# Latent attention with the plain and the rotated parts of queries and keys in tiles of their own

## The chip, the cores and the metric

The kernel runs on one core of one Trainium2 chip. The metric is the time on the device in microseconds (us), the median of several runs. All data are float32.

## What is computed

The reference is a model of three blocks over 512 tokens of width 1024; only the mixer of the last block matters here. It projects the normalised tokens to a compressed query `cq` (384), a compressed key and value `ckv` (256), a rotated key `kr` (32, shared by all heads), the queries, keys and values of a dilated attention, and two gates. Latent attention over 8 heads, and the merge behind it, cut from the reference:

```
q = (rms_norm(cq, q_norm_g) @ w_uq).reshape(B, S, 8, 64 + 32)
q = concatenate([q[..., :64], rope(q[..., 64:])])
k_rope = rope(kr)                                    # one for all heads
k_nope = (c_kv @ w_uk).reshape(B, S, 8, 64)
v_a    = (c_kv @ w_uv).reshape(B, S, 8, 64)
k_a = concatenate([k_nope, broadcast(k_rope)])
o_a = dense_attention(q, k_a, v_a)                   # softmax(q k / sqrt(96)) v, no mask
merged = gates[0] * (o_a @ w_branch_a) + gates[1] * (o_b @ w_branch_b)
return merged @ w_out
```

## The kernel before

One program with an instruction stream written out by hand for each engine; the engines meet by counting semaphores (`wait_ge`, `then_inc`). Activations lie transposed, 128 channels by 512 tokens a tile. Weights come through a ring of six units of 1 MB, loaded by SyncE in a fixed order (`mixer_units` for the mixer). `lin_open` takes the two PSUM banks 0 and 1 in turn, and waits until VectorE has emptied the tile before last (`lin_free`). Every logical float32 product is issued as two matmul instructions.

The order around the change: the input projections of the mixer (lines 1147 to 1177), dilated attention (1179 to 1188), the projections of latent attention (1191 to 1216), its attention loop (1219 to 1230), the product with the second branch's weights (`branch`, 1232), and the output projection.

Projections of latent attention: `head_query` (1191) makes one head's 96 query rows with three logical products; VectorE copies them to `HT[0:96, h]` (line 1379) and, two heads behind, rotates them with `rope` (1396 to 1405, a shuffle and three tensor operations over all 96 rows, with an angle of zero in the plain rows). Four key tiles (1212), two heads each, are copied in two halves to `KT` (2223, 2225). GpSimd copies the rotated key under each of the eight heads' plain keys (2882). The values are four token tiles of two logical products each (524), copied by 1392.

The attention loop (`attention`, 738) has 32 jobs: for each pair of heads, four blocks of 128 queries, and the two heads in turn. A job is: scores (one logical product over 96 rows, line 1222, into bank 4 + job mod 4); their maximum on VectorE (1561, 1571); exponentials on ScalarE (2458), which free the bank; a reciprocal and a scaling on VectorE (1581, 1584); four transposes on TensorE (760, `turn`); and their copy by ScalarE (2471). Two jobs' scores are issued ahead, in front of the transposes of the even job. VectorE takes the maximum of job u+1, then scales job u, then takes what a fill or a pair of heads left (`take_done`, 1599). Behind every eight jobs, a pair of heads is multiplied with its values (810, two column groups side by side), one job into the next eight; ScalarE's copy of the first transposes of the next heads waits for it. `fill` puts a tile of the product with the first branch's weights (539, eight instructions) in front of the transposes of jobs 3, 7, ..., 31; VectorE multiplies it with its gate (1461).

In the dilated attention the loop is the same, with scores of 64 rows, even heads in partitions 0 to 63 and odd ones in 64 to 127 (1181), and with half a gate tile (554, eight instructions) in front of every job's transposes.

```
                        if u % 2 == 0 and u + 2 < len(jobs):
                            scores(u + 2)
                            scores(u + 3)
                        if u or not lead:
                            fill(u)
                        if u % (2 * TT) == 1 and u > 2 * TT:
                            head_pair_values(u // (2 * TT) - 1)
                        turn(u)
```

Of the kernel before, what the change touches and what calls it, by code (L numbers as in the profile page):

```python
# [20 lines left out]
P = 128  # L21
# [24 lines left out]
DA_BRANCH = (12, 13, 14, 14, 15)  # L46
FF = 2816
# [118 lines left out]
def shape_constants():  # L166
# [21 lines left out]
    freq[64:80, 2] = -inv3  # L188
    freq[80:96, 2] = inv3
# [18 lines left out]
def build_program(nc, A, out):  # L208
    with ExitStack() as ctx:
# [30 lines left out]
        CQ, CKV, KR, ROPEM = BIG[:, 0:3, :], BIG[:, 3:5, :], BIG[0:DQK, 5, :], BIG[:, 6:8, :]  # L240
        KT, VA, MB = BIG[:, 16:24, :], BIG[:, 8:12, :], BIG[:, 0:8, :]
# [180 lines left out]
        def _(pe):  # L422
# [83 lines left out]
            def project(w, nk, width, rhs, ring_name, m=P, h_wait=False):  # L506
# [231 lines left out]
            def attention(heads, score, nkeys, ahead, maps, values, taken, fill, lead=None):  # L738
# [5 lines left out]
                def scores(u):  # L744
# [7 lines left out]
                    mm.then_inc(Q["sc_ready"], now.inc("sc_ready"))  # L752

# [23 lines left out]
                for u in range(ahead):  # L777
                    scores(u)
                for u in range(len(jobs)):
# [7 lines left out]
                    else:  # L787
                        if u % 2 == 0 and u + 2 < len(jobs):
                            scores(u + 2)
                            scores(u + 3)  # L790
                        if u or not lead:
                            fill(u)
                        if u % (2 * TT) == 1 and u > 2 * TT:
                            head_pair_values(u // (2 * TT) - 1)
                        turn(u)
                if maps == 2:
                    head_values(heads - 1)
                else:
                    head_pair_values(heads // 2 - 1)
# [360 lines left out]
            project(unit(), KD, 96, HT, "lin_ready", m=96)  # L1160
# [30 lines left out]
            def head_query(w, h):  # L1191
                wv = w[:, 0:3 * 384].rearrange("p (k c) -> p k c", k=3)
                ps = lin_open()
                for k in range(3):
                    mm = pe.matmul(ps[0:DQK, :], wv[:, k, h % 4 * DQK:(h % 4 + 1) * DQK], CQ[:, k, :],
                                   start=k == 0, stop=k == 2)
                mm.then_inc(Q["lin_ready"], now.inc("lin_ready"))

            w = unit()
            for h in range(4):  # L1200
                head_query(w, h)
            unit_used("lin_ready")
            w = unit()
            for h in range(4, 8):
                head_query(w, h)
                if h == 7:
                    unit_used("lin_ready")
            w = unit()[:, 0:2 * 512].rearrange("p (k c) -> p k c", k=2)
            for t in range(4):
                ps = lin_open()  # L1210
                for k in range(2):
                    mm = pe.matmul(ps, w[:, k, t * P:(t + 1) * P], CKV[:, k, :], start=k == 0, stop=k == 1)
                mm.then_inc(Q["lin_ready"], now.inc("lin_ready"))
                if t == 3:
                    unit_used("lin_ready")
            project_tokens(unit(), 2, 512, CKV)
            pe.wait_ge(Q["kr_copied"], now.next("kr_copied", MLA_H))

            def mla_score(o, h, m, qb):
                if qb == 0:  # L1220
                    pe.wait_ge(Q["roped"], KR_ROPES + h + 1)
                return pe.matmul(o, HT[0:DQK, h, qb * P:(qb + 1) * P], KT[0:DQK, h, :], start=True, stop=True)
# [6 lines left out]
            at["mla"] = now.count("lin_ready")  # L1229
# [10 lines left out]
        def _(v):  # L1240
# [306 lines left out]
            def attention(heads, nkeys, maps, scale, mask, L, head_done, take_fill, between=lambda u: None, sooner=()):  # L1547
# [50 lines left out]
                maxima(0)  # L1598
                def take_done(u):
# [569 lines left out]
            store_scaled(BIG[:, 5:6, :], 1, rows=DQK)  # L2169
# [30 lines left out]
            for s in range(2):  # L2200
                quarter_sums(g + 4 + s, quarters=token_quarters(DV, s))
                scale_tokens(DV, s)
                if s == 0:
                    rope(KR, SWAP_16, ROPEM[0:DQK, 0, :], ROPEM[0:DQK, 1, :], TURN[0:DQK, 0:S])
# [8 lines left out]
            def rope_head(h):  # L2213
                rope(HT[0:DQK, h, :], SWAP_16, ROPEM[0:DQK, 0, :], ROPEM[0:DQK, 1, :], TMP[0:DQK, 0, :])
# [5 lines left out]
            for t in range(MLA_H // 2):  # L2220
                ps = lin_take()
                v.wait_ge(*now.prev())
                v.tensor_copy(KT[0:HD, 2 * t, :], ps[0:HD, :]).then_inc(Q["dve_step"], now.inc("dve_step"))
                v.wait_ge(*now.prev())
                v.tensor_copy(KT[0:HD, 2 * t + 1, :], ps[HD:P, :]).then_inc(Q["lin_free"], now.inc("lin_free"))
                if t % 2:
                    rope_head(6 + t // 2)
            store_tokens(VA, 1, 512)
            v.wait_ge(Q["g_exp"], now.next("g_exp", 2 * KD))

            def take_branch_fill(u):
                if u % 4 == 3:
                    first_branch(MB, u // 4, KD + u // 4)
            attention(MLA_H, lambda qb: S, 1, float(DQK) ** -0.5, None, 0, pair_done(HT), take_branch_fill)
# [36 lines left out]
        def _(act):  # L2271
# [418 lines left out]
            mla = fill_order(MLA_H, 1, lambda u: u % 4 == 3)  # L2690
# [28 lines left out]
        def _(pool):  # L2719
# [158 lines left out]
            pool.wait_ge(Q["pos2_landed"], 32)  # L2878
# [157 lines left out]
```

## Time and profile before

| | us |
|---|---|
| median of three runs | 3076.05 |
| lowest and highest of them | 3075.49, 3081.58 |
| the profiled execution | 3078.61 |
| its span in the trace | 3076.9 |
| TensorE busy | 2957.9 (96%) |
| VectorE busy | 1326.0 (43%) |
| ScalarE busy | 652.8 (21%) |
| GpSimd busy | 844.5 (27%) |

The span is that of the instructions; the execution's own time is 1.7 us longer. In the page and its views PE is TensorE and PEld its weight loads, which run beside its matmuls; DVE is VectorE, ACT ScalarE, POOL GpSimd. L1222 is line 1222 of the kernel. Matmuls are pipelined: one of 512 columns lasts 0.59 us in the records, but the next starts 0.43 us after it. A number in brackets at the end of a row is the time for which the engine sat idle before it, and what released it. PEclk is the clock granted to TensorE, as a share of full speed.

### The profile page before, as it was taken

What the parts mean: (1) busy time and instruction counts of PE and PEld (TensorE: products, weight loads), DVE (VectorE), ACT (ScalarE), POOL (GpSimd) and SP (SyncE); (2) the same over time, 40 slices, a digit from 0 to 9 for tenths busy, and PEclk for the clock granted to TensorE, in tenths of its full rate; (3) what the DMA queues carried; (4) which work ended last, traced back from release to release, by engine and by line L of the source; (5) the groups of instructions that cost most, each with busy time, mean ns of one, the idle gap of its engine ahead of it and who ended that gap; (6) DMA issues with size and microseconds to landing.
All of it is one profiled execution on the core that took longest, in us unless ns stands there. A gap on an engine that the chain in (4) does not pass through costs nothing.

```text
span 3076.9 us, 31525 instructions
## 1 busy us (share of the span) xinstructions
PE 2957.9 (96%) x12406; PEld 1865.7 (61%) x12406; DVE 1326.0 (43%) x2202; ACT 652.8 (21%) x1055; POOL 844.5 (27%) x641
## 2 busy tenths in 40 slices
PE   9999998999999999989998999999999999999998
PEld 7865464333468654633333688887664345688887
DVE  6733543111546335431224644443563564544442
ACT  2035313111210253231112300002112341300011
POOL 5400021322134000222222154443400002345442
PEclk9999999999999999999999999999999999999999
DMA  4211124999522101249996122222221111122220
GB/s 185 83 69 42 42 88 181 389 384 386 217 82 83 69 28 55 74 148 384 379 379 276 69 93 85 82 96 82 91 77 45 68 42 55 69 83 96 82 96 28
DMA packets 81380, 412.65 MB, mean 134 GB/s; under 512 B 25872, under 2 KB 26256, under 8 KB 34768
## 3 DMA queue, kind: packets, MB, share of 16 engines
q1 hardware_dynamic: 56608, 387.54, 33.2%
q0 software_dynamic: 24624, 23.08, 2.3%
q8 instruction: 99, 1.62, 0.2%
q14 instruction: 49, 0.40, 0.0%
HBM read 513.28 MB, written 31.46 MB: 177 GB/s over the span
## 4 chain that ended last, share of the span: by engine, by line
PE 86%; DVE 8%; ACT 4%; issue 1%; DMA 1%; POOL 0%; SPq 0%; DVEq 0%; ACTq 0%; POOLq 0%
PE PS L998 37%; PE PS L937 11%; PE PS L554 6%; PE PS L539 5%; PE PS L959 5%; PE PS L628 4%; PE PS L514 3%; PE PS L1138 3%; PE PS L911 1%; PE PS L760 1%; PE PS L810 1%; PE PS L477 1%; PE PS L819 1%; PE PS L703 1%; DVE ATT L1511 1%
## 5 line engine op out<-in xcount | busy, mean ns | idle before, releaser
L2814 POOL TENSOR_TENSOR ATT<-ring 128x512 f32<-128x512 f32 (+1 forms) x98 | 129.4, 1320 | 1138.5 <-PE PS L998 710.7
L998 PE MATMUL PS<-G,ring 128*128 128x256 f32 x1360 | 321.6, 379 | 0.0
L998 PE MATMUL PS<-G,ATT 128*128 128x256 f32 x1232 | 291.4, 379 | 0.0
L998 PE MATMUL PS<-HT,ring 128*128 128x256 f32 x1264 | 287.6, 379 | 3.4 <-ACT HT L2367 1.8
L998 PEld LDWEIGHTS PS<-G,ring 128*128 128x128 f32 x1360 | 258.4, 190 | 35.1
L998 PEld LDWEIGHTS PS<-HT,ring 128*128 128x128 f32 x1264 | 239.7, 190 | 40.3 <-issue 4.0
L2538 ACT ACTIVATE TMP<-PS 128x256 f32<-128x256 f32 x92 | 35.3, 384 | 1053.5 <-PE PS L998 936.2
L998 PEld LDWEIGHTS PS<-G,ATT 128*128 128x128 f32 x1232 | 234.1, 190 | 32.7 <-issue 0.7
L937 PE MATMUL PS<-ring,G 128*64 128x512 f32 x1024 | 226.8, 595 | 2.5 <-ACT G L2507 2.5
L554 PE MATMUL PS<-HT,ring 128*128 128x512 f32 x448 | 205.4, 601 | 0.0
L2822 POOL TENSOR_TENSOR ATT<-ring 128x512 f32<-128x512 f32 (+1 forms) x98 | 173.4, 1769 | 7.7
L1839 DVE TENSOR_TENSOR G<-PS,G 128x256 f32<-128x256 f32 x48 | 20.4, 424 | 343.5 <-ACT G L2513 343.3
L998 PE MATMUL PS<-HT,ATT 128*128 128x256 f32 x696 | 164.6, 379 | 0.0
L1910 DVE TENSOR_TENSOR BIG<-PS,TMP 128x256 f32<-128x256 f32 x100 | 42.4, 424 | 260.5 <-ACT TMP L2538 257.6
L937 PEld LDWEIGHTS PS<-ring,G 128*64 128x64 f32 x1024 | 70.7, 137 | 135.9 <-issue 132.9
L998 PEld LDWEIGHTS PS<-HT,ATT 128*128 128x128 f32 x696 | 132.1, 190 | 18.3 <-issue 0.5
L554 PEld LDWEIGHTS PS<-HT,ring 128*128 128x128 f32 x448 | 80.7, 190 | 101.6 <-issue 96.2
L1910 DVE TENSOR_TENSOR G<-PS,TMP 128x256 f32<-128x256 f32 x42 | 17.8, 424 | 270.1 <-ACT TMP L2538 265.1
L2816 POOL TENSOR_TENSOR ATT<-ring 128x512 f32<-128x512 f32 (+1 forms) x98 | 133.5, 1363 | 0.0
L2756 POOL DMA_INDIRECT expert_rows<-G,ATT x46 | 46.6, 1013 | 311.0 <-DVE G L1850 310.6
L2819 POOL TENSOR_TENSOR ring<-ATT,ring 128x512 f32<-128x512 f32 (+1 forms) x98 | 128.8, 1314 | 7.7
L959 PE MATMUL PS<-ring,G 128*64 128x512 f32 x512 | 116.0, 594 | 10.2 <-DVE G L1832 5.9
(363 smaller groups left out, 4483.9 us busy)
## 6 DMA issues: line engine op xcount, KB each, us to landing
ring<-in_stream SPq DMA_DIRECT2D x163, 1024.0 KB, 4.8
ring<-in_experts_gu SPq DMA_DIRECT2D x128, 1024.0 KB, 8.8
ring<-in_experts_down SPq DMA_DIRECT2D x64, 1024.0 KB, 8.7
G<-expert_rows SPq DMA_DIRECT2D x8, 1024.0 KB, 7.6
h_tokens<-G POOLq DMA_DIRECT2D x2, 2048.0 KB, 7.6
XT<-in_xT SPq DMA_DIRECT2D x1, 1024.0 KB, 8.7
G<-in_pT POOLq DMA_DIRECT2D x2, 512.0 KB, 6.3
out_T<-XT SPq DMA_DIRECT2D x2, 512.0 KB, 3.7
```

The source lines that it names most:

```text
L514: mm = pe.matmul(ps[0:m, :], wv[:, k, c:c + m], rhs[:, k, :], start=k == 0, stop=k == nk - 1)
L539: mm = pe.matmul(ps, w[:, k, c:c + P], rhs[:, k, :], start=k == 0, stop=k == nk - 1)
L554: mm = pe.matmul(units["ps"], w[:, k, c:c + P], rhs[:, k, :], start=k == 0, stop=k == KD - 1)
L628: mm = pe.matmul(product(g, name), y[:, k, s * P:(s + 1) * P], x[:, k * 256:(k + 1) * 256], start=k == 0 and name in ("P1", "P2", "P3", "P ...
L937: mm = pe.matmul(PS[r, 4 + q % 2, :], XGT[:, q % 2, k * P + CAP * side:k * P + CAP * (side + 1)], ws[side][:, kk * 512:(kk + 1) * 512], st ...
L959: mm = pe.matmul(PS[r, n, :], HIDT[:, q % 2, j * P + CAP * side:j * P + CAP * (side + 1)], ws[side][:, j * D + n * 512:j * D + (n + 1) * 512],
L998: mm = pe.matmul(product(g, name), x[:, k * P:(k + 1) * P], y[:, k, :], start=first and k == 0 and name in ("P1", "P2", "P3", "P5"), stop= ...
L1138: mm = pe.matmul(ps, w[:, k, m % 2 * P:(m % 2 + 1) * P], HP[:, k, :], start=k == 0, stop=k == KD - 1)
L2814: pool.tensor_tensor(a["S1"], a["A21"], a["A22"], ALU.add)\
L2816: pool.tensor_tensor(a["S3"], a["A11"], a["A21"], ALU.subtract)\
L2819: pool.tensor_tensor(a["S2"], a["S1"], a["A11"], ALU.subtract)\
L2822: pool.tensor_tensor(a["S4"], a["A12"], a["S2"], ALU.subtract)\
```

## The change

The weights of the queries are reordered on the host into a unit of rotated columns (8 heads by 32) and a unit of plain columns (8 heads by 64). The queries become two tiles of rotated rows (`QT`, four heads each) and four of plain rows (`QN`, two heads each); keys become four plain tiles (`KN`) and one tile `KEY` that holds the rotated key four times over, once in each 32 rows (the key's columns are repeated in its weights). The scores of a job are two products that add up in PSUM: 64 plain rows and 32 rotated rows, and `two_scores` issues the plain products of two jobs, then the rotated ones. The values are projected behind the first two jobs' scores (`early`). The fills go in front of the transposes of the jobs in `MLA_BRANCH`, the last behind the transposes of job 31. The first tile of the second branch waits for the last heads only in front of its last product.

```diff
+MLA_BRANCH = (4, 9, 13, 17, 21, 25, 29, 31)
...
 def mixer_units(w_in, w_uq, w_uk, w_uv, w_a, w_b, w_o):
+    key = np.tile(w_in[:, QR + KVR:QR + KVR + ROPE_M], (1, P // ROPE_M))
+    heads = w_uq.reshape(QR, MLA_H, DQK)
+    turned = heads[:, :, NOPE:].reshape(QR, MLA_H * ROPE_M)
+    plain = heads[:, :, :NOPE].reshape(QR, MLA_H * NOPE)
...
-         unit_of(w_in, 0, D, 576, 672)]
+         unit_of(key, 0, D, 0, P)]
...
-    return (u + cut(w_uq, 384) + cut(w_uk, 512) + cut(w_uv, 512)
+    return (u + cut(turned, MLA_H * ROPE_M) + cut(plain, MLA_H * NOPE) + cut(w_uk, 512) + cut(w_uv, 512)
...
-        CQ, CKV, KR, ROPEM = BIG[:, 0:3, :], BIG[:, 3:5, :], BIG[0:DQK, 5, :], BIG[:, 6:8, :]
-        KT, VA, MB = BIG[:, 16:24, :], BIG[:, 8:12, :], BIG[:, 0:8, :]
+        CQ, CKV, KR, ROPEM = BIG[:, 0:3, :], BIG[:, 3:5, :], BIG[:, 5, :], BIG[:, 6:8, :]
+        KN, VA, MB = BIG[:, 16:20, :], BIG[:, 8:12, :], BIG[:, 0:8, :]
+        QN, QT, KEY = HT[:, 0:4, :], HT[:, 4:6, :], HT[:, 6, :]
...
+                        if late and c == 0 and k == nk - 1:
+                            pe.wait_ge(*late)
...
+                def two_scores(u):
+                    for part in score:
+                        for n in (u, u + 1):
+                            if part is score[0] and n >= 4:
+                                pe.wait_ge(Q[taken], base[taken] + n - 3)
+                            h, qb = jobs[n]
+                            mm = part(PS[:, 4 + n % 4, 0:nkeys(qb)], h, 0, qb)
+                            if part is score[-1]:
+                                mm.then_inc(Q["sc_ready"], now.inc("sc_ready"))
...
-                for u in range(ahead):
-                    scores(u)
+                if early:
+                    two_scores(0)
+                    early()
+                else:
+                    for u in range(ahead):
+                        scores(u)
...
-                            scores(u + 2)
-                            scores(u + 3)
-                        if u or not lead:
+                            if early:
+                                two_scores(u + 2)
+                            else:
+                                scores(u + 2)
+                                scores(u + 3)
+                        last = early and u == len(jobs) - 1
+                        if (u or not lead) and not last:
                             fill(u)
                         if u % (2 * TT) == 1 and u > 2 * TT:
                             head_pair_values(u // (2 * TT) - 1)
                         turn(u)
+                        if last:
+                            fill(u)
...
-            project(unit(), KD, 96, HT, "lin_ready", m=96)
+            project(unit(), KD, P, HT, "lin_ready")
...
-            w = unit()
-            for h in range(4):
-                head_query(w, h)
...
-            project_tokens(unit(), 2, 512, CKV)
-            pe.wait_ge(Q["kr_copied"], now.next("kr_copied", MLA_H))
...
+            project(unit(), 3, MLA_H * ROPE_M, CQ, "lin_ready")
+            project(unit(), 3, MLA_H * NOPE, CQ, "lin_ready")
+            project(unit(), 2, MLA_H * NOPE, CKV, "lin_ready")
+
+            def plain_score(o, h, m, qb):
+                r = slice(NOPE * (h % 2), NOPE * (h % 2 + 1))
+                return pe.matmul(o, QN[r, h // 2, qb * P:(qb + 1) * P], KN[r, h // 2, :], start=True, stop=False)
+
+            def turned_score(o, h, m, qb):
+                if qb == 0 and h == 0:
+                    pe.wait_ge(Q["kr_copied"], now.next("kr_copied"))
+                if qb == 0 and h % 4 == 0:
+                    pe.wait_ge(Q["roped"], KR_ROPES + h // 4 + 1)
+                r = slice(ROPE_M * (h % 4), ROPE_M * (h % 4 + 1))
+                return pe.matmul(o, QT[r, h // 4, qb * P:(qb + 1) * P], KEY[r, :], start=False, stop=True)
...
-                if u % 4 == 3:
-                    project_tile(b, 4, 512, DQ, u // 4)
+                if u in MLA_BRANCH:
+                    project_tile(b, 4, 512, DQ, MLA_BRANCH.index(u))
...
-            attention(MLA_H, mla_score, lambda qb: S, 2, 1, pair_values(VA), "e_ready", branch_fill)
-            drained("lin_ready")
-            branch(HT[:, 0:4, :])
+            attention(MLA_H, (plain_score, turned_score), lambda qb: S, 2, 1, pair_values(VA), "e_ready", branch_fill,
+                      early=lambda: project_tokens(unit(), 2, 512, CKV))
+            paired = now.count("lin_ready")
+            project(unit(), 4, 512, HT[:, 0:4, :], "lin_ready", late=(Q["lin_free"], paired))
+            project(unit(), 4, 512, HT[:, 0:4, :], "lin_ready")
...
                 maxima(0)
+                if early:
+                    early()
...
-            for h in range(MLA_H):
-                store(HT[:, h:h + 1, :], 1, rows=DQK)
-                if h >= 2:
-                    rope_head(h - 2)
...
+            store(QT, 2)
+            for i in range(2):
+                rope(QT[:, i, :], SWAP_16, ROPEM[:, 0, :], ROPEM[:, 1, :], TMP[:, 0, :])
+                store(QN[:, 2 * i:2 * i + 2, :], 2)
+            store(KN, MLA_H // 2)
...
-            for h in range(MLA_H):
-                pool.tensor_copy(KT[NOPE:DQK, h, :], KR[NOPE:DQK, :]).then_inc(Q["kr_copied"], now.inc("kr_copied"))
+            pool.tensor_copy(KEY, KR).then_inc(Q["kr_copied"], now.inc("kr_copied"))
```

The angles of the rotation are laid out for all four groups of 32 rows, and VectorE takes the fills, and the values' four tiles (behind the maximum of job 0), in the order of TensorE.

## Rows read from the trace of the kernel before

**Rows 1.** Page, part 1: busy time and share of the span of each engine.
```profile
PE 2957.9 (96%) x12406; PEld 1865.7 (61%) x12406; DVE 1326.0 (43%) x2202; ACT 652.8 (21%) x1055; POOL 844.5 (27%) x641
```
**Rows 2.** Window view: length, busy us of PE, PEld, DVE, ACT, POOL; clock, DMA share.
```profile
2426.70:2474.30 47.60, 38.03 (x82) 13.84 (x81) 36.67 (x61) 10.66 (x14) 4.49 (x8) 0.96 0.19 66
2474.30:2568.70 94.40, 87.75 (x320) 41.57 (x320) 56.14 (x140) 44.03 (x96) 0.00 (x0) 0.98 0.10 34
```
**Rows 3.** Timeline of VectorE, a query head: start, us, engine, line, operation.
```profile
2438.42 0.69 DVE L1379 COPY HT<-PS 96x512 f32<-96x512 f32 x1
...
2439.15 0.72 DVE L1399 STREAM_SHUFFLE TMP<-HT 96x512 f32<-96x512 f32 x1
...
2442.14 0.69 DVE L1379 COPY HT<-PS 96x512 f32<-96x512 f32 x1
```
**Rows 4.** Timeline of TensorE: a query head that waited, and the first transposes.
```profile
2442.88 2.81 PE L1195 MATMUL PS<-BIG,ring 128*96 128x512 f32 x6 [0.49 <-DVE HT L1379]
...
2478.22 0.66 PE L760 MATMUL PS<-MATS,ATT 128*128 128x128 f32 x4 [0.23 <-DVE ATT L1584]
```
**Rows 5.** Timeline of TensorE, dilated attention: transposes, scores, gate tile, transposes.
```profile
2294.89 0.60 PE L760 MATMUL PS<-MATS,ATT 128*128 128x128 f32 x4
2295.42 1.13 PE L1181 MATMUL PS<-BIG 64*128 64x512 f32 x4
2296.48 3.70 PE L554 MATMUL PS<-HT,ring 128*128 128x512 f32 x8
2300.02 0.60 PE L760 MATMUL PS<-MATS,ATT 128*128 128x128 f32 x4
```
**Rows 6.** Timeline of TensorE, latent attention, jobs 8 to 13.
```profile
2497.60 0.60 PE L760 MATMUL PS<-MATS,ATT 128*128 128x128 f32 x4
2498.13 3.65 PE L810 MATMUL PS<-ATT,BIG 128*64 128x512 f32 x16
2501.72 0.66 PE L760 MATMUL PS<-MATS,ATT 128*128 128x128 f32 x4
2502.21 1.88 PE L1222 MATMUL PS<-BIG,HT 96*128 96x512 f32 x4
2504.23 0.63 PE L760 MATMUL PS<-MATS,ATT 128*128 128x128 f32 x4
2504.70 3.60 PE L539 MATMUL PS<-BIG,ring 128*128 128x512 f32 x8
2508.13 0.60 PE L760 MATMUL PS<-MATS,ATT 128*128 128x128 f32 x4
2508.57 1.88 PE L1222 MATMUL PS<-BIG,HT 96*128 96x512 f32 x4
2510.29 0.60 PE L760 MATMUL PS<-MATS,ATT 128*128 128x128 f32 x4
2511.44 0.63 PE L760 MATMUL PS<-MATS,ATT 128*128 128x128 f32 x4 [0.55 <-DVE ATT L1584]
```
**Rows 7.** Timeline of ScalarE and VectorE: a copy behind the values product, a maximum.
```profile
2501.88 0.60 ACT L2471 ACTIVATE ATT<-PS 128x512 f32<-128x512 f32 x1 [4.31 <-PE PS L810]
...
2509.63 0.69 DVE L1561 TENSOR_REDUCE SM<-PS 128x1 f32<-128x512 f32 x1 [0.41 <-PE PS L1222]
```
**Rows 8.** Window view, columns as in group 2: jobs 29 and 30, and behind them.
```profile
2554.80:2558.20 3.40, 1.64 (x11) 1.11 (x10) 2.13 (x7) 2.75 (x6) 0.00 (x0) 1.00 0.00 0
2558.30:2561.70 3.40, 3.40 (x5) 1.35 (x4) 0.51 (x2) 0.51 (x1) 0.00 (x0) 0.50 0.00 0
```
**Rows 9.** Timeline of TensorE, the end of latent attention and the second branch.
```profile
2557.87 5.29 PE L539 MATMUL PS<-BIG,ring 128*128 128x512 f32 x8
2563.00 0.60 PE L760 MATMUL PS<-MATS,ATT 128*128 128x128 f32 x4
2564.29 3.65 PE L810 MATMUL PS<-ATT,BIG 128*64 128x512 f32 x16 [0.69 <-ACT ATT L2471]
2568.74 0.70 PE L514 MATMUL PS<-HT,ring 128*128 128x512 f32 x1 [0.79 <-DVE HT L1626]
```

More of the change, by code:

```diff
@@ L187, in shape_constants @@
             freq[b + h:b + h + 8, 1] = sign * inv2
-    freq[64:80, 2] = -inv3
-    freq[80:96, 2] = inv3
+    for b in range(0, P, ROPE_M):
+        freq[b:b + 16, 2] = -inv3
+        freq[b + 16:b + 32, 2] = inv3
     rev = np.zeros((P, NG + NE), np.float32)
@@ L504, in late_sum, with project @@
                     .then_inc(Q["late_sum"], now.inc("late_sum"))
-            def project(w, nk, width, rhs, ring_name, m=P, h_wait=False):
+            def project(w, nk, width, rhs, ring_name, m=P, h_wait=False, late=None):
                 wv = w[:, 0:nk * width].rearrange("p (k c) -> p k c", k=nk)
@@ L736, in stick_breaking, with attention @@
                 now.skip("w_ready", SB_H)
-            def attention(heads, score, nkeys, ahead, maps, values, taken, fill, lead=None):
+            def attention(heads, score, nkeys, ahead, maps, values, taken, fill, lead=None, early=None):
                 jobs = attention_jobs(heads, maps)
@@ L1189, in _ @@
             pe.wait_ge(Q["h_ready"], now.next("h_ready", (QR + KVR) // P))
[L1191 to L1197, printed above, removed]
-            w = unit()
@@ L1200, in _ @@
-            for h in range(4):
-                head_query(w, h)
[L1202 to L1215, printed above, removed]
@@ L1216, in _ @@
-            project_tokens(unit(), 2, 512, CKV)
-            pe.wait_ge(Q["kr_copied"], now.next("kr_copied", MLA_H))
[L1219 to L1222, printed above, removed]
+            project(unit(), 3, MLA_H * ROPE_M, CQ, "lin_ready")
+            project(unit(), 3, MLA_H * NOPE, CQ, "lin_ready")
+            project(unit(), 2, MLA_H * NOPE, CKV, "lin_ready")
@@ L1224, in _ @@
             b = {}
             def branch_fill(u):
-                if u % 4 == 3:
-                    project_tile(b, 4, 512, DQ, u // 4)
-            at["mla"] = now.count("lin_ready")
-            attention(MLA_H, mla_score, lambda qb: S, 2, 1, pair_values(VA), "e_ready", branch_fill)
-            drained("lin_ready")
-            branch(HT[:, 0:4, :])
+                if u in MLA_BRANCH:
+                    project_tile(b, 4, 512, DQ, MLA_BRANCH.index(u))
+            at["mla"] = now.count("lin_ready") + TT
@@ L1545, in stick_breaking, with attention @@
                 now.skip("lw_ready", SB_H)
-            def attention(heads, nkeys, maps, scale, mask, L, head_done, take_fill, between=lambda u: None, sooner=()):
+            def attention(heads, nkeys, maps, scale, mask, L, head_done, take_fill, between=lambda u: None, sooner=(), early=None):
                 jobs = attention_jobs(heads, maps)
@@ L2168, in _ @@
             store_scaled(CKV, 2)
-            store_scaled(BIG[:, 5:6, :], 1, rows=DQK)
+            store_scaled(BIG[:, 5:6, :], 1)
             begin_sum("lin_free", QR // P + KVR // P + 1)
@@ L2203, in _ @@
                 if s == 0:
-                    rope(KR, SWAP_16, ROPEM[0:DQK, 0, :], ROPEM[0:DQK, 1, :], TURN[0:DQK, 0:S])
+                    rope(KR, SWAP_16, ROPEM[:, 0, :], ROPEM[:, 1, :], TURN[:, 0:S])
             def take_gate_fill(u):
@@ L2212, in _ @@
             at["dil_done"] = now.count("lin_free")
-            def rope_head(h):
-                rope(HT[0:DQK, h, :], SWAP_16, ROPEM[0:DQK, 0, :], ROPEM[0:DQK, 1, :], TMP[0:DQK, 0, :])
-            for h in range(MLA_H):
-                store(HT[:, h:h + 1, :], 1, rows=DQK)
-                if h >= 2:
-                    rope_head(h - 2)
[L2220 to L2229, printed above, removed]
-            def take_branch_fill(u):
-                if u % 4 == 3:
-                    first_branch(MB, u // 4, KD + u // 4)
-            attention(MLA_H, lambda qb: S, 1, float(DQK) ** -0.5, None, 0, pair_done(HT), take_branch_fill)
+            store(QT, 2)
[3 more added lines that the diff above has]
+            store(KN, MLA_H // 2)
+            def take_branch_fill(u):
+                if u in MLA_BRANCH:
+                    m = MLA_BRANCH.index(u)
+                    if m == 0:
+                        v.wait_ge(Q["g_exp"], now.next("g_exp", 2 * KD))
+                    first_branch(MB, m, KD + m)
+            attention(MLA_H, lambda qb: S, 1, float(DQK) ** -0.5, None, 0, pair_done(HT), take_branch_fill,
+                      early=lambda: store_tokens(VA, 1, 512))
             at["mla_done"] = now.count("lin_free")
@@ L2689, in _ @@
             dil = fill_order(MLA_H, 1, lambda u: u % 2)
-            mla = fill_order(MLA_H, 1, lambda u: u % 4 == 3)
+            mla = fill_order(MLA_H, 1, lambda u: u in MLA_BRANCH)
             attention(MLA_H, lambda qb: S, 1, 1.0, True,
```

1 line of the change is left out of this document (removed).

## The prediction

> **What bounds the kernel now.** I read the page first: TensorE is busy 2957.9 us, 96% of the span [rows 1], so an edit counts only where it shortens or lengthens what TensorE issues, or where it starts or ends a wait of TensorE. Then the window view of the two stages that the diff touches. In the projections of latent attention, 2426.7 to 2474.3, TensorE is busy 38 of 47.6 us; in the attention loop, up to the second branch, 87.8 of 94.4 us [rows 2]. The first stage has slack that isn't TensorE's. The VectorE timeline says why: one head of the queries costs it a copy and a four-step rotation, 3.72 us from copy to copy (2438.42 to 2442.14) [rows 3], while TensorE needs six instructions of 0.43 us, 2.6 us; it starts the next head when VectorE has freed a bank: the product at 2442.88 waited for the copy that began at 2442.14 [rows 3, 4]. So VectorE sets the pace there. In the loop TensorE mostly sets it, with waits for the softmax of the next job where nothing stands in front of its transposes: 2510.29 to 2511.44 where 0.44 would do [rows 6].
>
> **The projections.** Removed: eight heads of six instructions, replaced by two rotated and four plain tiles of six each; the four key tiles (four instructions each) stay; the values' 16 instructions go behind the first scores. That leaves 52 instructions by 0.43, 22.4 us. VectorE has 10 copies by 0.73 (the step from copy to shuffle [rows 3]) and two rotations by 3.0 (3.72 less the copy), 13.3 us: it no longer sets the pace, and each rotation stands where two banks cover it. The wait for the last copy stays, about 1 us (0.79 is idle and some 0.2 is uncovered behind the last heads' copy [rows 9]). The first scores then start at 2426.7 + 22.4 + 1.0 = 2450.1, where now they start at 2474.3.
> GpSimd copies the rotated key once instead of eight times, and starts when the dilated heads are copied, 20 us before the first scores need it. The key unit has 128 columns instead of 96: still 16 instructions, and copies of 96 rows take 0.69 us [rows 3], as those of 128 do. Units of weights and DMAs stay equal in number. All this at nothing.
>
> **The opening of the loop.** Scores of jobs 0 and 1, 2.1 us; the values, 16 by 0.43, 6.9; then jobs 2 and 3 beside VectorE's last value copy, the maximum of job 1 and the scaling of job 0: 0.2 + 0.73 + 1.0 + 0.8 = 2.7 us. The first transpose comes at 2450.1 + 2.1 + 6.9 + 2.7 = 2461.8, where now it comes at 2478.2 [rows 4]: **16.4 us earlier**.
>
> **The scores.** Now a pair of jobs is four instructions, 1.72 us (2508.57 to 2510.29) [rows 6]. After, it is a pair of 64-row products and a pair of 32-row products. The 64-row form is in the trace: the dilated branch's scores take two row groups side by side, four instructions in 1.06 us, and with them transposes to transposes take 5.13 us (2294.89 to 2300.02) [rows 5], against 0.44 + 3.43 = 3.87 without [rows 6]. So the pair costs 1.26: two steps of 0.43, and 0.40 for two changes of tile height, 0.20 each. If the 32-row pair runs side by side too, a pair of jobs costs 0.86 + 0.86 + 3 x 0.20 = 2.32 us, 0.60 more than now. Nothing in the trace goes from 64 rows straight to 32: between nothing and 0.30, I take the 0.20 of the other two changes. Both ends stay in the range: 16 pairs, 3.2 us less or 1.6 more.
> The Trainium skill (TensorEngine Tiling (Array Packing), Key Properties) says that a change of tiling mode, not of the tile alone, drains TensorE; this case's trace agrees for 128 to 64 and back, 0.20 us each, and by the rule the third change costs the same; without it the forecast would be 3 us lower.
> Fourteen pairs lie behind the first transpose: 14 x 0.60 = **8.4 us more**.
>
> **The waits in the loop.** Of jobs u and u+1 (u even), the transposes of u+1 need VectorE to have taken the maximum of job u+2 first, since that stands ahead in its queue. From that maximum to the transposes it is 1.81 us (2509.63 to 2511.44) [rows 6, 7]. Now the score of u+2 is ready 0.86 us before its partner's, and the wait is 0.71. After, both of a pair end together, so the maximum starts some 0.1 us behind the start of job u's transposes: u+1 starts 1.9 us after u, a wait of 1.45. And there are more such places. A weight product stands in front of jobs 3, 7, 11, ... now, and a values product in front of 9, 17, 25; what is bare is 5, 13, 21. The new list puts the products in front of 9, 13, 17, ..., in three cases right beside the values product; bare are 3, 7, 15, 23 and 11, 19, 27. At the last three VectorE also has two copies to do (branch tile and heads, 0.73 each) ahead of the maximum, behind a scaling that itself waited for ScalarE, which waits out the values product (4.31 us [rows 7]): about 2.4 us each. After: 4 x 1.45 + 3 x 2.4 = 13.0. Before: 3 x 0.71, and three times 0.30 behind the values product (2502.21 to 2504.23 less 1.72) [rows 6], 3.0, the latter now covered by longer scores. Jobs 30 and 31 wait about 2 us either way. Difference **10.0 us more**.
>
> **The end.** The last weight product moves behind the last transposes, where the values now wait 1.29 - 0.53 = 0.8 us, and three quarters of the first branch tile run before the last heads are copied, where 4.45 - 3.59 = 0.9 us is idle [rows 6, 9]. **1.7 us less.** VectorE and GpSimd start their next work with the same copy, so later stages only shift.
>
> **The clock.** The last weight product took 5.13 us (2557.87 to 2563.00) [rows 9] instead of 3.43: for 3.4 us the granted clock was 0.50, right behind a stretch in which TensorE was busy 1.64 of 3.40 us [rows 8]. That 1.7 us goes, as the jobs shift; but the new bare places (three of 2.4 us, the end, the opening) are as thin. Between none and five dips; I take two, at 1.7 each, since a dip needs the thin part to fall right: net **1.7 us more**.
>
> **Sum.** -16.4 + 8.4 + 10.0 - 1.7 + 1.7 = +2.0 us. The profiled execution took 3078.6 us, so 3080.6 for it; the median of the runs shown is 3076.05, 2.6 lower, and there I forecast 3078.1. A measurement of this kernel can tell about 0.2%, 6.2 us, from no change: this is no change, the gain of the projections given back in the loop. The case's own range: no third change of height and no dip, 3076.05 + 2.0 - 3.2 - 3.4 = 3071.5; the dear change and five dips, 3076.05 + 2.0 + 1.6 + 5.1 = 3084.7.
>
> **Rivals.** Faster: the loop hides what it gains in work. If successive products of different height follow without a change, and the copies of VectorE fall before the three long waits (each then 1.45), the sum is -16.4 + 7.1 - 1.7 - 1.7 = -12.7, 3063 us. For it: the pace of now has slack on VectorE (56 of 94 us busy [rows 2]). Against: the 0.20 is plain in the trace, and the order of VectorE's queue is fixed.
> Slower, first: the change doesn't do what it says, and the 32-row pair does not run side by side. Then each pair costs 0.86 more, 16 x 0.86 = 13.8, which no wait absorbs, as VectorE's wait counts from their end: 3092 us. It decides once over half of the pairs run in turn (7 us). For it: no 32-row product is in the trace. Against: the 64-row ones pair perfectly.
> Slower, second: the thin places make the clock fall each time: five dips instead of two, and with a dear third change 3084. The trace has it once in a like place.
>
> **How the numbers follow.** Forecast 0.50, faster rival 0.25, 32 rows in turn 0.12, clock 0.13. Faster by over 0.2% (below 3069.9): the rival and 0.02 of the forecast's low end, 0.27. Slower (above 3082.2): the other two and a little, 0.26. The likeliest case alone is 3071.5 to 3084.7; the range goes from 3061, under the faster rival, to 3087, and leaves out the row groups in turn and little else.
>
> **What would show it.** Right: the projections end near 2449 with TensorE without a gap; a score pair of eight instructions takes 2.3 us; job 11's transposes wait 2.4 us behind VectorE's copies; the second branch starts at about its old time, near 2567. Wrong: score pairs near 1.8 or 3.2 us, or transposes of jobs 3, 7, 11 that do not wait.

## The result, and the profile after

The changed kernel took 3088.64 us (median of seven runs, 3082.44 to 3090.14), beside 3076.17 us for the kernel before in the same runs. The ratio is 1.0032, with a 95% interval of 1.0022 to 1.0042: **slower by about 10 us** (the two medians alone lie 12.5 us apart). On the median of 3076.05 shown ahead of the prediction the ratio gives 3085.9 us (3082.8 to 3089.0); the forecast was 3078.1 us in a range of 3061 to 3087. That is inside the range, 1.1 us below its upper end, with an interval that reaches past it, and outside the likeliest case of 3071.5 to 3084.7. No change was forecast and a small loss came; the rival of the falling clock is what happened, at a higher price than I gave it.

The page of the changed kernel, its span, part 1 and the clock of part 2, answers to [rows 1]:

```profile
span 3086.1 us, 31578 instructions
PE 2966.5 (96%) x12458; PEld 1865.9 (60%) x12458; DVE 1307.0 (42%) x2166; ACT 652.4 (21%) x1055; POOL 840.8 (27%) x634
PEclk9999999999999999999999999999999989999999
```

VectorE has 19 us less to do, as intended, and TensorE is 9 us longer busy with 52 more instructions of 12,458. The windows of the projections up to the first scores, and of the loop from the first transposes to the second branch, answer to [rows 2]. The columns are length, busy us of PE, PEld, DVE, ACT and POOL, mean clock, and DMA:

```profile
2423.40:2446.80 23.40, 22.55 (x54) 9.76 (x53) 13.21 (x21) 10.63 (x14) 0.61 (x1) 1.00 0.26 90
2458.60:2577.00 118.40, 102.71 (x369) 42.53 (x369) 53.12 (x133) 42.44 (x92) 0.00 (x0) 0.88 0.06 22
```

Of the kernel before, the projections are the 47.6 us of [rows 2], which hold the values' 16 instructions as well, and the loop alone is this window:

```profile
2478.20:2568.70 90.50, 84.08 (x312) 40.14 (x312) 53.79 (x134) 42.48 (x92) 0.00 (x0) 0.98 0.07 24
```

The projections are pure TensorE now (22.55 of 23.40 us busy). The loop grew from 90.5 to 118.4 us, and its mean clock fell from 0.98 to 0.88. The granted clock was at half for 27.3 us of it, in four falls of 3.4 to 10.2 us, where before there was one of 3.4 [rows 8]. The first four windows here lie within these falls, which began in or just behind the waits of jobs 11, 15, 19 and 23 (columns as above):

```profile
2493.20:2500.00 6.80, 6.80 (x15) 2.47 (x14) 3.40 (x11) 2.60 (x6) 0.00 (x0) 0.50 0.00 0
2507.00:2510.20 3.20, 3.20 (x10) 1.37 (x11) 1.29 (x4) 1.48 (x5) 0.00 (x0) 0.50 0.00 0
2524.20:2534.20 10.00, 9.61 (x21) 4.24 (x22) 4.72 (x13) 3.01 (x8) 0.00 (x0) 0.50 0.00 0
2541.20:2547.80 6.60, 6.60 (x15) 2.56 (x14) 2.99 (x8) 1.19 (x3) 0.00 (x0) 0.50 0.02 4
2559.80:2566.40 6.60, 6.60 (x24) 2.96 (x25) 4.43 (x12) 2.75 (x6) 0.00 (x0) 1.00 0.00 0
```

The last line is the stretch behind job 27, which waits 2.52 us like jobs 11 and 19: the clock stays full there, as it does behind jobs 1, 3, 7 and 31.

What it looks like from job 8 to job 13, in the timeline of TensorE, beside [rows 6] (L1226 plain products, L1234 rotated ones, L779 transposes, L548 branch tile, L839 values):

```profile
2478.90 0.66 PE L779 MATMUL PS<-MATS,ATT 128*128 128x128 f32 x4
2479.40 3.60 PE L548 MATMUL PS<-BIG,ring 128*128 128x512 f32 x8
2482.93 3.65 PE L839 MATMUL PS<-ATT,BIG 128*64 128x512 f32 x16
2486.51 0.66 PE L779 MATMUL PS<-MATS,ATT 128*128 128x128 f32 x4
2487.10 1.13 PE L1226 MATMUL PS<-BIG,HT 64*128 64x512 f32 x4
2488.16 1.13 PE L1234 MATMUL PS<-HT 32*128 32x512 f32 x4
2489.22 0.66 PE L779 MATMUL PS<-MATS,ATT 128*128 128x128 f32 x4
2492.39 0.63 PE L779 MATMUL PS<-MATS,ATT 128*128 128x128 f32 x4 [2.52 <-DVE ATT L1598]
2492.95 1.84 PE L1226 MATMUL PS<-BIG,HT 64*128 64x512 f32 x4
2494.72 2.08 PE L1234 MATMUL PS<-HT 32*128 32x512 f32 x4
2496.73 1.11 PE L779 MATMUL PS<-MATS,ATT 128*128 128x128 f32 x4
2497.63 4.81 PE L548 MATMUL PS<-BIG,ring 128*128 128x512 f32 x8
2502.28 0.60 PE L779 MATMUL PS<-MATS,ATT 128*128 128x128 f32 x4
```

Job 11's transposes (2492.39) wait 2.52 us for VectorE; behind that wait the same score pair that took 2.12 us (2487.10 to 2489.22) takes 3.78 (2492.95 to 2496.73), and the branch tile 4.65 instead of 3.43. The timeline of VectorE shows what stands ahead of the maximum of job 12 (2490.57), behind a scaling (2488.39) that was late itself:

```profile
2488.20 0.16 DVE L1595 RECIPROCAL SM<-SM 128x1 f32<-128x1 f32 x1 [6.55 <-ACT ATT L2466]
2488.39 0.49 DVE L1598 TENSOR_SCALAR ATT<-ATT,SM 128x512 f32<-128x512 f32 x1
2488.99 0.69 DVE L1475 TENSOR_TENSOR BIG<-PS,G 128x512 f32<-128x512 f32 x1
2489.78 0.69 DVE L1643 COPY HT<-PS 128x512 f32<-128x512 f32 x1
2490.57 0.69 DVE L1575 TENSOR_REDUCE SM<-PS 128x1 f32<-128x512 f32 x1
```

### The profile page after: what moved, and what is told of

It is laid out like the page before. It is cut to its first block, busy times and chain, and to the rows that moved or that the text cites. A ratio compares the mean times of both kernels' runs of the same rounds, so it can differ in the third digit from the quotient of the medians.

```text
span 3086.1 us, 31578 instructions
## 1 busy us (share of the span) xinstructions
PE 2966.5 (96%) x12458; PEld 1865.9 (60%) x12458; DVE 1307.0 (42%) x2166; ACT 652.4 (21%) x1055; POOL 840.8 (27%) x634
## 4 chain that ended last, share of the span: by engine, by line
PE 87%; DVE 7%; ACT 4%; issue 1%; DMA 1%; POOL 0%; SPq 0%; DVEq 0%; ACTq 0%; POOLq 0%
PE PS L1027 37%; PE PS L966 11%; PE PS L563 6%; PE PS L548 6%; PE PS L988 5%; PE PS L523 4%; PE PS L637 4%; PE PS L1167 3%; PE PS L940 1%; PE PS L779 1%; PE PS L839 1%; PE PS L484 1%; PE PS L848 1%; PE PS L712 1%; DVE ATT L1525 1%
```

## The experiments

Two theories stood after the result. A: the new list of fills leaves TensorE bare in front of too many odd jobs; the waits cost time themselves, and the thin stretches bring the clock down. B: it is the new score products, of 64 and 32 rows, that bring the clock down, whatever stands around them.

A table first. The loop is from the first transposes (job 0) to the first instruction of the second branch; "waits" is TensorE's time behind VectorE's scaling, with the wait of job 0, from the view of waits; "half" is the time in the loop at half clock, added up from windows of 0.5 us; the clock is the mean of the loop. These columns are of one profile each. The ratio is to the kernel before, in the same runs. Below, differences are between medians; from the changed kernel they come out 2 to 4 us smaller by the ratios (experiment 2: 9 instead of 12.7), since its ratio of 1.0032 is smaller than that of the two medians, 1.0041.

| kernel | median us | ratio (95% interval) | loop us | waits us | half us | clock |
|---|---|---|---|---|---|---|
| before | 3076.2 | | 90.5 | 4.8 | 3.4 | 0.98 |
| changed | 3088.6 | 1.0032 (1.0022 to 1.0042) | 118.4 | 16.1 | 27.3 | 0.88 |
| 1 old list | 3074.7 | 0.9994 (0.9985 to 1.0003) | 102.1 | 8.4 | 10.2 | 0.95 |
| 2 bare places filled | 3076.0 | 1.0003 (0.9994 to 1.0012) | 105.2 | 0.7 | | 1.00 |
| 3 before, new list | 3088.3 | 1.0041 (1.0028 to 1.0055) | 100.9 | 12.8 | 6.8 | 0.97 |
| 4 unpaired scores | 3140.6 (one run) | | 164.0 | 2.3 | 92.2 | 0.72 |
| 5 halves | 3061.9 | 0.9953 (0.9939 to 0.9966) | 91.4 | 2.6 | | 1.00 |
| 6 halves, copies moved | 3060.4 | 0.9948 (0.9935 to 0.9962) | 89.2 | 1.3 | | 1.00 |
| 7 before, halves | 3073.5 | 0.9991 (0.9982 to 1.0000) | 86.0 | 1.7 | | 1.00 |
| 8 copies moved alone | 3078.9 | 1.0007 (0.9997 to 1.0016) | 106.5 | 12.3 | 10.2 | 0.95 |
| 9 halves, values first | 3061.8 | 0.9953 (0.9937 to 0.9970) | 91.4 | 2.8 | | 1.00 |
| 10 filled, 32 rows | 3086.5 | 1.0033 (1.0020 to 1.0045) | 117.0 | 0.4 | 20.5 | 0.91 |

**1. The old list of fills on the changed kernel.**

```diff
-MLA_BRANCH = (4, 9, 13, 17, 21, 25, 29, 31)
+MLA_BRANCH = (3, 7, 11, 15, 19, 23, 27, 31)
```

> The changed kernel with the fills back in front of jobs 3, 7, 11, ..., 27 (the last stays behind job 31's transposes). Theory A (the list leaves TensorE bare in front of too many odd jobs, and the bare places lower the clock): the waits before jobs 3, 7, 11, 15, 19, 23, 27 go, those before 5, 13, 21, 29 come: some 7 us less waiting, and with thin places of 1.3 us only, most of the 27 us at half clock go, worth up to 13 us. 3065 to 3071 us, faster than before. Theory B (the score products of 64 and 32 rows, whatever stands around them, bring the clock down): only the 7 us of waits go and the half clock stays: 3079 to 3082 us.

It fell between the two theories: 3074.66 us, 14 less than the changed kernel, but no faster than before. The waits halved (7.7 us less), and the clock rose from 0.88 to 0.95, 17 us less at half clock. Two falls remain, behind job 13 and behind jobs 29 to 31; behind job 13 one bare job with a wait of 1.26 us was enough:

```profile
2497.03 0.65 PE L779 MATMUL PS<-MATS,ATT 128*128 128x128 f32 x4
2498.95 0.63 PE L779 MATMUL PS<-MATS,ATT 128*128 128x128 f32 x4 [1.26 <-DVE ATT L1598]
2499.51 2.08 PE L1226 MATMUL PS<-BIG,HT 64*128 64x512 f32 x4
2501.51 2.08 PE L1234 MATMUL PS<-HT 32*128 32x512 f32 x4
```

So the list is the larger part of the loss, and a wait as short as this can be followed by a fall. It need not be: jobs 5 and 21 wait 1.26 us in the same profile, and the clock stays full behind them.

**2. The bare places filled with idle products.** The results are overwritten by the transposes that follow, so the output stays.

```diff
+BARE = {1: (512,), 3: (512, 256), 7: (512, 256), 15: (512, 256), 23: (512, 256),
+        11: (512,) * 3, 19: (512,) * 3, 27: (512,) * 3, 31: (512, 512)}
...
+                    if early:
+                        for width in BARE.get(u, ()):
+                            pe.matmul(PS[:, 2 + u % 2, 0:width], IDENT, KN[:, 0, 0:width], start=True, stop=True)
                     pe.wait_ge(Q["p_ready"], now.next("p_ready"))
```

> The changed kernel with idle products (identity by a key tile, result overwritten by the transposes) in front of the transposes of the bare jobs, sized to the waits seen in the trace: 1 to 3 logical products of 0.86 us. Nothing else moves and no wait on VectorE gets shorter. Theory A: TensorE has no thin place left, the clock stays at full, and the time falls by what the half clock cost beside nothing else, 10 to 13 us, to 3075 to 3079 us. Theory B: the score products are as they were, so the clock still falls: 3086 to 3092 us. If I mis-sized the fillers, at most 2 us more.

3075.95 us, 12.7 less. Hardly anything but the clock's fall was made shorter: a filled job starts at most 0.1 us sooner than a bare one, some 0.5 us over the loop. The window of the loop:

```profile
2457.60:2562.80 105.20, 104.69 (x408) 44.45 (x408) 53.13 (x133) 42.44 (x92) 0.00 (x0) 1.00 0.07 25
```

The clock is full throughout, with the same score products. The half clock thus cost 118.4 - 105.2 = 13.2 us of the loop, near half of its 27.3 us. Theory A holds, and B in its strict form (whatever stands around them) falls.

**3. The new list on the kernel before.**

```diff
-                if u % 4 == 3:
-                    project_tile(b, 4, 512, DQ, u // 4)
+                if u in MLA_BRANCH:
+                    project_tile(b, 4, 512, DQ, MLA_BRANCH.index(u))
```

(and the same for VectorE and ScalarE, with the list of the change)

> The kernel before with only the new list of fills (jobs 4, 9, 13, ..., 31), scores of 96 rows as they were. Theory A: bare are 3, 7, 15, 23 (0.7 to 1.3 us) and 11, 19, 27 (about 2.8 us each, VectorE has two copies ahead): 8 us of waits more, and the three long ones bring the clock down, 3 to 10 us more: 3086 to 3093 us. Theory B: 8 us of waits and no further half clock, since no score product has 64 or 32 rows: 3083 to 3085 us, one dip as before.

3088.32 us: the list alone costs 12 us, as much as the whole change. Job 11 waits 2.74 us, and behind it the score pair takes 2.60 us (2507.80 to 2510.40) instead of 1.72:

```profile
2503.98 0.63 PE L761 MATMUL PS<-MATS,ATT 128*128 128x128 f32 x4
2507.34 0.63 PE L761 MATMUL PS<-MATS,ATT 128*128 128x128 f32 x4 [2.74 <-DVE ATT L1585]
2507.80 2.80 PE L1223 MATMUL PS<-BIG,HT 96*128 96x512 f32 x4
2510.40 1.06 PE L761 MATMUL PS<-MATS,ATT 128*128 128x128 f32 x4
```

The time lies in theory A's range, but most of it is the waits themselves: 8.0 us more of them, in a loop that is 10.4 us longer. The clock fell only twice, behind jobs 11 and 27, 3.4 us each time, one fall more than before; the changed kernel has 27.3 us at half clock with the same places bare. So B has a part: between scores of 96 rows, with waits of 12.8 us in place of 16.1, the clock was down for a quarter of the time. The waits are not quite the same, and the falls are read from one profile each, so the scores' part is not measured by itself here.

**4. The scores unpaired.**

```diff
-                    for part in score:
-                        for n in (u, u + 1):
+                    for n in (u, u + 1):
+                        for part in score:
```

> The changed kernel with each job's two products in a row (plain u, rotated u, plain u+1, rotated u+1) instead of both plain ones first. If the row groups run side by side and each change of height costs 0.2 us, a pair of jobs now takes 4 x 0.86 + 4 or 5 changes = 4.3 to 4.4 us instead of the 2.1 of the trace, and 16 pairs add some 35 us: 3115 to 3125 us. If changes of height were free but the side by side were real: 3.4 a pair, 3106 to 3112. If nothing ran side by side, nothing changes.

3140.56 us. At full clock a pair takes 4.2 us (2462.51 to 2466.72), near the expected 4.3, twice the 2.12 of the paired order: row groups do run side by side, and each change of height costs 0.2. The other 17 us, beyond the expected 35, are the clock: 92.2 us at half instead of 27.3 cost some 32 us, and some 14 us of waits vanish behind the longer scores. In the first window here TensorE is busy throughout at full clock; in the second, right behind it, it is busy for all of 17.1 us and at half clock for all of it (transposes, single score products, most of a branch tile). Two lines of its timeline follow:

```profile
2457.80:2471.00 13.20, 13.20 (x35) 4.81 (x33) 7.67 (x19) 3.53 (x8) 0.00 (x0) 1.00 0.22 79
2471.10:2488.20 17.10, 17.10 (x25) 6.15 (x25) 3.48 (x10) 2.75 (x6) 0.00 (x0) 0.50 0.01 1
2474.62 2.07 PE L1226 MATMUL PS<-BIG,HT 64*128 64x512 f32 x2
2476.62 2.07 PE L1234 MATMUL PS<-HT 32*128 32x512 f32 x2
```

**5. The fills in halves.** Each tile of the first branch is made in two halves of four instructions, in front of the transposes of 15 odd jobs, and the last behind job 31.

```diff
-MLA_BRANCH = (4, 9, 13, 17, 21, 25, 29, 31)
+MLA_BRANCH = (3, 7, 13, 17, 21, 25, 29, 31)
+MLA_HALVES = (1, 3, 5, 7, 11, 13, 15, 17, 19, 21, 23, 25, 27, 29, 31, 32)
...
+            def branch_half(units, rhs, n):
...
+                if half == 0:
+                    units["ps"] = lin_open()
+                for k in (2 * half, 2 * half + 1):
+                    mm = pe.matmul(units["ps"], w[:, k, c:c + P], rhs[:, k, :], start=k == 0, stop=k == 3)
+                if half:
+                    mm.then_inc(Q["lin_ready"], now.inc("lin_ready"))
```

> The changed kernel with the weight products of the first branch cut into halves of four instructions, one in front of the transposes of nearly every odd job (1, 3, 5, 7, 11, 13, ..., 31) and the last behind job 31. A half lasts 1.7 us, the bare waits 1.1 to 1.4: theory A says that they vanish, but for 0.3 to 0.8 us before jobs 11, 19, 27, where VectorE has the heads' copy ahead, and that no thin place is left to lower the clock. Against the run with the old list (3074.7, with 8 us of waits and 10 us at half clock in this stage) 8 to 12 us less: 3063 to 3067 us. Rival: the score pair itself, now 2.12 us with its rotated half on half of the rows, keeps the clock falling even without waits: 3070 to 3076.

3061.87 us, 0.47% under the kernel before: faster than both, and 1 us better than expected. No wait above 0.9 us is left, and the clock stays full in the loop with the same score pairs:

```profile
2457.20:2548.60 91.40, 89.24 (x369) 37.30 (x369) 53.15 (x133) 42.49 (x92) 0.00 (x0) 1.00 0.08 29
```

**6. VectorE's copies moved as well.**

```diff
                         maxima(u + 1)
+                    if early and u in (10, 18, 26):
+                        take_done(u)
                     normalise(u)
```

> As the halves, and VectorE takes the pair of heads (and the branch tile) between the maximum of the next job and the scaling of jobs 10, 18, 26, where it idles for ScalarE, instead of behind the scaling. Theory: the copies leave the path of the maximum of jobs 12, 20, 28, and the rest of the wait before 11, 19, 27 goes: 0 to 2.4 us less than the halves alone; if ScalarE's exponential came earlier than I think, the scaling is late instead and nothing is gained.

The loop is 2.2 us shorter (91.4 to 89.2), as expected. The medians differ by 1.5 us, with intervals that overlap: as a time of the whole kernel that is not shown.

**7. The halves on the kernel before.** The same `branch_half`, at the places of the kernel before, with the last tile ahead of jobs 30 and 31; VectorE and ScalarE take the finished tiles by the first of these lists.

```diff
+MLA_BRANCH = (3, 7, 13, 17, 21, 25, 29, 31)
+MLA_HALVES = (1, 3, 5, 7, 11, 13, 15, 17, 19, 21, 23, 25, 27, 29, 30, 31)
...
-                if u % 4 == 3:
-                    project_tile(b, 4, 512, DQ, u // 4)
+                if u in MLA_HALVES:
+                    branch_half(b, DQ, MLA_HALVES.index(u))
```

> The kernel before, scores of 96 rows and its own projections, with the halves alone (two of them in front of jobs 30 and 31). It waits 5.5 us for VectorE in the loop and loses 1.7 to the clock: theory A says 5 to 7 us less than before, 3069 to 3072 us. The difference to the changed kernel with halves then is what the new projections and scores are worth by themselves: 16 to 17 us of projections against 16 pairs x 0.4 us of scores and less hiding at the start, so some 7 us in favour of the change. If halves are worth the same on both sides and no more, the new products are worth nothing.

3073.51 us, 3.4 less than the kernel before where I had expected 5 to 7, and at the edge of a difference (the loop is 4.5 us shorter). It is 11.6 us behind the changed kernel with halves: the change's tiles are worth that once their loop is filled; I had expected 7.

**8. The copies moved alone, fills as in the change.** The edit is the one of experiment 6, on the changed kernel:

```diff
+                    if early and u in (10, 18, 26):
+                        take_done(u)
```

> The changed kernel, fills as it has them, with only VectorE's two copies moved between the maximum and the scaling of jobs 10, 18, 26. Theory: the waits before jobs 11, 19, 27 go from 2.52 to 1.26 us as before 15 and 23, 3.8 us less, and the three thinnest places become like the others, so some of the 27 us at half clock goes, between nothing and 10 us of time: 3075 to 3085 us. If the copies aren't what lengthens these waits, nothing changes: 3088.

3078.9 us, 10 less than the change, for three pairs of copies. Job 11's wait is half of what it was:

```profile
2494.51 0.66 PE L779 MATMUL PS<-MATS,ATT 128*128 128x128 f32 x4
2496.43 0.63 PE L779 MATMUL PS<-MATS,ATT 128*128 128x128 f32 x4 [1.25 <-DVE ATT L1598]
```

Waits fell by 3.8 us, and the time at half clock by 17 us. Two falls are left, one of them behind the wait of job 1, which was followed by none in the changed kernel's profile.

**9. The values before the first scores, with halves.** (VectorE's copies of the values likewise.)

```diff
-            at["mla"] = now.count("lin_ready") + TT
+            project_tokens(unit(), 2, 512, CKV)
+            at["mla"] = now.count("lin_ready")
...
-                      early=lambda: project_tokens(unit(), 2, 512, CKV))
+                      early=lambda: None)
```

> The kernel with halves, but with the values projected in front of the first scores, as before the change. TensorE then waits once for the last value's copy instead of the last key's, and the maximum and exponential of jobs 0 and 1 and the scores of 2 and 3 no longer lie beside the values: jobs 0 and 1 start later by the chain of the first job, 1 to 3 us. 3063 to 3065 us. If the move is worth nothing, 3062, the same as the halves.

3061.8 us, and the loop of 91.4 to the tenth: in a filled loop, projecting the values behind the first scores is worth nothing measurable. My expectation of 1 to 3 us was wrong: the first transposes come 35.3 us behind the start of the projections in both orders, since either way TensorE waits 0.88 us for VectorE's last copy ahead of the first scores, and then for the scaling of job 0: for 0.44 us with the values behind the first scores, where that scaling stands behind the last value copy and the maximum of job 1, and for 0.62 us with the values ahead, where the whole softmax of job 0 stands behind the scores.

**10. The bare places filled with products of 32 rows.**

```diff
-                            pe.matmul(PS[:, 2 + u % 2, 0:width], IDENT, KN[:, 0, 0:width], start=True, stop=True)
+                            pe.matmul(PS[:, 2 + u % 2, 0:width], IDENT[0:32, :], KN[0:32, 0, 0:width], start=True, stop=True)
```

> The kernel with idle products in the bare places, but over 32 rows instead of 128: TensorE is busy for the same time (each filler adds two changes of tile height, some 0.3 us, of which the waits hold little: up to 2 us over the nine places), with a quarter of the array. If it is enough for the clock that TensorE is busy, the loop stays at full clock as with the full fillers: 3076 to 3079 us. If what matters is how much of the array works, the clock falls as it does with the bare waits: 3084 to 3091 us. The unpaired scores point to the second: there it fell over 100 us while TensorE never waited long.

3086.45 us. TensorE's records are all but without a gap (116.68 of 117.00 us), the waits are 0.4 us, and the clock falls all the same: three times, for 6.8 us each, behind the longest fillers (jobs 11, 19 and 27). The loop's window; the 10.3 us ahead of the first fall, with no idle time; then the filler of job 11 and the score pair behind it, which slows down:

```profile
2463.10:2580.10 117.00, 116.68 (x409) 47.85 (x409) 53.14 (x133) 42.49 (x92) 0.00 (x0) 0.91 0.06 22
2488.00:2498.30 10.30, 10.30 (x44) 4.05 (x42) 4.50 (x11) 4.32 (x10) 0.00 (x0) 1.00 0.00 1
2494.65 2.84 PE L781 MATMUL PS<-BIG,MATS 32*128 32x512 f32 x6
2497.42 0.66 PE L784 MATMUL PS<-MATS,ATT 128*128 128x128 f32 x4
2498.00 1.70 PE L1231 MATMUL PS<-BIG,HT 64*128 64x512 f32 x4
2499.64 2.08 PE L1239 MATMUL PS<-HT 32*128 32x512 f32 x4
```

One rival is left: a filler of 32 rows has a change of height at each end, which one of 128 rows has not, and makes the stretch 0.2 us longer. Whether the few rows or the changes of height let the clock fall, this pair of experiments does not tell.

## Why the prediction was right or wrong

**The projections: right.** TensorE went through its 52 instructions without a gap (22.5 us, forecast 22.4), and the first transposes came 35.3 us behind the start of the stage instead of 51.5: 16.2 us earlier, forecast 16.4.

**The score pair: right, a little cheaper.** 2.12 us from start to start, and 2.27 as the forecast of 2.32 counts it, from transposes to transposes less 0.44 (2486.51 to 2489.22); the 32-row pair runs side by side. The change straight from 64 to 32 rows, which no row of before showed, costs 0.20: from the plain pair's start to the rotated pair's it is 1.06 us, two steps of 0.43 and the change. The Trainium skill's rule (TensorEngine Tiling (Array Packing), Key Properties), that every change of mode drains TensorE, names no price here; it agrees with these 0.20 us in that the third change costs about as much as the other two. Whether the time is a drain or the weight load of 0.19 us, which at a change does not run ahead, no run tells.

**The waits: right.** Jobs 3, 7, 15 and 23 wait 1.26 us by the records and 11, 19 and 27 wait 2.52 (start to start 1.92 and 3.18; forecast 1.9, and 2.4 + 0.44, some 2.8), 1 us more over the three long ones; job 31 waits 1.95. The chain is the one described: two copies ahead of the maximum, behind a scaling that waited for ScalarE.

**The end: right.** No gap is left between the last values and the second branch, as forecast.

**The clock: the term that failed.** I took two falls of 1.7 us for one that went, +1.7 net, and bounded it at five. The profile has four falls in the loop, within that bound, but they last 27.3 us together, 6.8 on average instead of 3.4, and cost 13.2 us (experiment 2), 3.3 each instead of 1.7. Less the 1.7 us of the one before that is +11.5 net: 3.4 us more for two falls more, and 6.4 for their length. That makes 9.8 us, and with it the forecast of +2.0 becomes +11.8; measured are 11.6 us in the profiles between the start of the stage (2426.7 before, 2423.4 after) and the second branch (2568.7 and 2577.0). The last sign named ahead, a second branch near 2567, is the one that failed. The rest of the difference in span is 3.3 us upstream, where the changed kernel's profile reached the stage sooner, and 0.9 us after it, later; the profiles of all kernels here differ by more at the start of the stage (2421.9 to 2428.2), so neither is put down to the change.

"A dip needs the thin part to fall right" fits what came: of nine bare places with waits of 1.1 to 2.5 us four were followed by a fall. What was at fault is the price of one, taken from the only fall of before [rows 8], whose stretch holds a product of full height. The stretch behind a bare job here holds a score pair whose rotated half works on 64 of 128 rows, and experiments 3, 4 and 10 point to that: between 96-row scores each of the two falls lasted 3.4 us. So the rival named as "clock", five dips of 1.7 us or 8.5, came true in kind with four, at 13.2 us; and theory B of the experiments, false in its strict form, names what lengthens the falls, as far as these runs tell.

**The direction.** The gain of the projections was given back in the loop, as forecast, and 10 us beyond it. The list of fills gave back more (experiment 1: 14 us) than the products did (experiment 7 against 5: in a filled loop the change gains 11.6 us).

**Open.** Stretches with narrow products brought the clock down without idle time in these mixtures; how narrow they must be, and whether it is the rows or the changes of height between them, was not measured. Nor is it known why, of equal waits, some were followed by a fall and some not. Nor was a loop with scores of 96 rows tried behind the projections of the change.

## What to carry to other kernels

When work between two dependent instructions of the busiest engine is moved, list every place that it covered, before and after: here each of eight fills covered an odd job; in the new list three stand beside a product that covers the same job anyway and one in front of an even job that needs none, and that cost more than the new tiles saved. Many small covers beat few large ones: the same products in halves of 1.7 us, sized to the waits, turned a loss of 0.3% into a gain of 0.5%. And a wait of TensorE can cost more than its length, when the clock falls behind it: here 16.1 us of waits came with 13.2 us of slower clock. A copy that is "somewhere in the queue" belongs in the slot in which its engine idles; three pairs of them, moved by one instruction, were worth 10 us where the places were bare, and 2 us of the loop where they were filled.

## What the runs showed of the hardware

- TensorE's granted clock fell to half while its records show it busy without a gap: in experiment 4 behind 13.2 us of full clock, for 17.1 us, with single products of 64 and of 32 rows, and in experiment 10 behind fillers of 32 rows, where fillers of 128 rows in the same places (experiment 2) kept it full. The Trainium skill (TensorE: Matmul & The Clock Gate, Part 1) puts the clock down to how busy the engine was of late; by these traces the busy time of the records alone doesn't decide it, and the measurement decides.
- Waits of 1.1 to 2.7 us were followed by falls of 3.4 to 10.2 us at half clock, or by none: the same 2.52 us by a fall behind jobs 11 and 19 and by none behind job 27.
- Two products of 32 rows in different row groups run side by side at the pace of one: four instructions in 1.06 us, which is two steps of 0.43 and 0.20 for the change of height. A filler of six 32-row instructions took 2.77 us (2494.65 to 2497.42), six of 128 rows 2.58.
- The time at half clock ahead of this stage, in code that hardly differs, was 24 to 45 us over the profiles of all kernels here, and the stage started at 2421.9 to 2428.2 us, earliest in the profile with the least of it and latest in the one with the most. A change of a few us is to be read within its stage.
